# First block's norms in passes of high and low parts, with a buffer per tile; smaller sums, a swapped buffer and three moved waits in a decoder trunk

## The chip, the cores and the metric

The kernel runs on one core of a Trainium2 chip. The metric is the device time of one execution in microseconds (us), the median of several runs. Engines: PE (TensorE, matmul), DVE (VectorE), ACT (ScalarE), POOL (GpSimd) and SP (SyncE, which here only issues DMAs). Each has its own instruction stream; they meet at semaphores, each of which counts the finished instructions of one kind.

## The reference

One layer of a hybrid decoder trunk, in float32, over a prompt of 16 meta tokens and 2048 tokens, and over 8 samples of 4 tokens with a state each:

```python
h = rmsnorm(x, n1);  z = h @ w_in                       # 1024 -> 2560: u | q | f | i | gate
y_pool = pool_mix(z[..., :512])                         # window means 2, 4, 8, 16, then a product per group
y_rec = hgrn2_mix(z[..., 512:])                         # 4 heads of 128, chunked recurrence
x = x + concat(y_pool, y_rec) @ w_out
a, b = (rmsnorm(x, n2) @ w for w in (w_a, w_b))         # 1024 -> 2816
x = x + (gelu(conv3(a)) * b) @ w_down
y = rmsnorm(x, final_g)

def gla_chunk(S, q, k, g, v):                           # the recurrence of one chunk and head
    G = cumsum(g);  decay = exp(G[t] - G[s]) for s <= t
    A = einsum('td,sd,tsd->ts', q, k, decay)
    o = A @ v + (q * exp(G)) @ S
    S = exp(G[-1]) * S + (k * exp(G[-1] - G)).T @ v
```

Outputs are y of prompt and samples and the new states (pool, recurrent, convolution).

## The kernel before

**Blocks.** The prompt is worked in four blocks of 512 tokens, each of four tiles of 128. Block 0 (`hd` true, written out) also carries 48 head columns: the 16 meta tokens and the 32 sample tokens. Its 560 columns are split into a front (304: head and tiles 0 and 1) and a back (256: tiles 2 and 3), one PSUM bank each. Blocks 1 to 3 are a loop over the same code with `hd` false.

**Products in three parts.** A float32 product is made of reduced-precision parts: every operand is split in a high part (a cast) and a low part (value minus high), and PE does high x high, weight low x high, weight high x low (`three`, L558; `features`, L574, for a unit of eight k tiles). Weights come in 96 units of 128 x 1024 per block in four slots. In block 0 SP loads a unit raw, POOL splits it (L533 the high part, L536 the low), and SP stores the split to DRAM; later blocks load the split. A slot is loaded again once `unit_done` has counted the unit that used it.

**The norms.** ACT squares and sums the tokens, DVE and ACT make the reciprocal root, the tokens are scaled (`scaled`), PE transposes them (`row_transposes`, `token_rows`; L595), DVE multiplies the transposed tile by the gain out of PSUM into the buffer `t32` (L1608), ACT casts it to `h_hi` (L1145), and DVE subtracts for `h_lo` (L1616). There is one `t32` for all tiles and for the head, so a tile's multiply waits for the low part of the tile before. The head's counterparts are L603, L1630, L1150 and L1633. In block 0 the first user of the first norm is `first_gates` (L1085): the front halves of the four forget-gate units, unit by unit in three parts, then the back halves. The second norm's is `head_first` (L986), alike for the first four up-projection units. Both wait for tile 0's, tile 1's and the head's low parts before their first matmul.

**The gates.** DVE clamps each gate unit out of PSUM (L1730, L1731), ACT takes exponentials and logarithms, DVE cumulates (L1738 to L1743) and makes the keys; then come the decay operands, whose exponents DVE or, for heads 1 to 3 of block 0, POOL makes in the buffer `dec` (L378, L379).

**Attention.** 16 steps a block, a head and a tile each (`attention`, L737, L1953). For a step PE makes eight score matrices (L755, L758), DVE masks them (L1959) and adds the upper four to the lower four (L1965), PE multiplies the four sums by the values (L783), adds the state's share (L786) and the state's update (L789, whose keys ACT has copied, L1308, from a transpose, L771). DVE updates the state (L1975). A 128-column float32 product without split parts is two PE instructions. After certain steps PE does another unit: U and gate tiles (`gate_tile`, L819), pool products. Scores run two steps ahead; those of a head's first step wait for all its decay operands.

**Head states.** The samples' recurrent states of a head are loaded to one of two buffers `s0`, updated and stored (L1179). One buffer lies in the operands of odd heads, the other over `dec`; POOL's exponents of head 1 and ACT's first decays both wait for all four stores.

**Down projection.** Two halves of 512 columns. Each starts with the residual's add of what PE left in PSUM before (`half_residual`, L2024). In block 0, half 1 uses banks 3, 6, 7, 0 and 1; half 0 used 0, 1, 2, 5, 4. L1059 waits for the adds of tiles 0 and 1 (and the head) ahead of everything of half 1.

## Time and profile before

| | us |
| --- | --- |
| median of three runs (2640.07 to 2645.72) | 2641.01 |
| profiled execution, own time | 2635.29 |
| its span, first to last instruction | 2633.5 |
| PE busy | 2517.5 (96%) |
| DVE busy | 1178.2 (45%) |
| ACT busy | 714.2 (27%) |
| POOL busy | 450.8 (17%) |

The chain of work that ended last, followed back, is 88% PE, 6% DVE, 3% issue, 2% ACT and 1% DMA. The mean granted clock of PE is 0.985 of full speed. A row of a timeline gives start, duration, engine, line and operation, the count where several are merged, and in brackets the idle time before with what ended it. Matmuls are pipelined: their durations overlap, and what one costs is the distance of two starts. Between 30 and 34 us the granted clock is shown as 1.00 where the matmuls go at half pace; their distances are what is read there.

### The profile page before, as it was taken

To read this page: it belongs to the slowest core of one execution; us is meant where nothing else is said; L and a number is where in the kernel's file an instruction comes from. 1 tells how busy PE (TensorE), PEld (TensorE's weight loads), DVE (VectorE), ACT (ScalarE), POOL (GpSimd) and SP (SyncE) were. 2 spreads that over 40 slices of the span, in tenths; PEclk is the share of its full clock that TensorE was granted. 3 is DMA by queue.
4 is the path that set the end of the run, shared out by engine and by line. 5 is a ranking of instruction groups with operands and counts; after the bars stand their busy time and mean duration, and the time that the engine had idled before them with its cause. 6 is when DMAs were issued, how large, how long until landed. Compare 5 with 4: busy or idle time off the path is not lost.

```text
span 2633.5 us, 36805 instructions
## 1 busy us (share of the span) xinstructions
PE 2517.5 (96%) x13455; PEld 2135.5 (81%) x13455; DVE 1178.2 (45%) x2249; ACT 714.2 (27%) x1457; POOL 450.8 (17%) x331
## 2 busy tenths in 40 slices
PE   5997889999999999999999999999999999999997
PEld 5887779999777888888887887888887887888886
DVE  5977555333355764222236564322235764322234
ACT  3313222222323342211233332211133332211133
POOL 3625226555550120000000020000000020000000
PEclk9979989999999999999999999999999999999999
DMA  6641338777757423555656523455655622555653
GB/s 202 244 153 49 108 130 293 251 252 257 260 219 266 160 81 128 207 191 191 227 196 224 190 84 128 176 191 191 231 200 190 235 81 102 200 184 188 221 215 133
DMA packets 145354, 489.08 MB, mean 186 GB/s; under 512 B 8882, under 2 KB 79779, under 8 KB 96026
## 3 DMA queue, kind: packets, MB, share of 16 engines
q1 hardware_dynamic: 136747, 482.58, 50.5%
q10 hardware_dynamic: 8472, 4.75, 0.6%
q8 instruction: 80, 1.31, 0.2%
q14 instruction: 55, 0.44, 0.1%
HBM read 375.45 MB, written 112.02 MB: 185 GB/s over the span
## 4 chain that ended last, share of the span: by engine, by line
PE 88%; DVE 6%; issue 3%; ACT 2%; DMA 1%; POOL 0%; DVEq 0%; SPq 0%; ACTq 0%
PE ps L560 23%; PE ps L562 23%; PE ps L561 22%; PE ps L614 11%; PE ps L758 3%; PE ps L783 2%; PE ps L595 1%; DVE arena L1927 1%; DMA w_both<-w_split 1%; PE ps L789 1%; PE ps L755 0%; DVE arena L1959 0%; ACT arena L1157 0%; PE ps L840 0%; PE ps L786 0%
## 5 line engine op out<-in xcount | busy, mean ns | idle before, releaser
L560 PE MATMUL ps<-h_hi,w_both 128*128 128x512 f32 (+2 forms) x1664 | 626.6, 377 | 21.9 <-issue 13.5
L562 PE MATMUL ps<-h_lo,w_both 128*128 128x512 f32 (+2 forms) x1664 | 622.0, 374 | 0.0
L561 PE MATMUL ps<-h_hi,w_both 128*128 128x512 f32 (+2 forms) x1664 | 618.3, 372 | 0.0
L560 PEld LDWEIGHTS ps<-h_hi,w_both 128*128 128x128 f32 x1664 | 314.0, 189 | 78.2 <-issue 14.5
L562 PEld LDWEIGHTS ps<-h_lo,w_both 128*128 128x128 f32 x1664 | 314.1, 189 | 59.5
L561 PEld LDWEIGHTS ps<-h_hi,w_both 128*128 128x128 f32 x1664 | 314.5, 189 | 58.8
L560 PE MATMUL ps<-w_both,act_hi 128*128 128x512 f32 (+1 forms) x748 | 297.4, 398 | 4.3 <-DVE x_tok L2035 3.8
L562 PE MATMUL ps<-w_both,act_hi 128*128 128x512 f32 (+1 forms) x748 | 296.0, 396 | 0.0
L561 PE MATMUL ps<-w_both,act_lo 128*128 128x512 f32 (+1 forms) x748 | 295.6, 395 | 0.0
L614 PE MATMUL ps<-h_hi,w_both 128*128 128x304 f32 (+1 forms) x1664 | 290.2, 298 | 5.6 <-DVE arena L1731 2.4
L2112 DVE TENSOR_TENSOR act_lo<-arena,act_hi 128x512 fp32r<-128x512 f32 (+1 forms) x176 | 138.5, 789 | 331.3 <-ACT act_hi L1464 331.0
L378 POOL TENSOR_TENSOR arena<-arena 128x256 f32<-128x256 f32 x63 | 45.2, 717 | 1338.6 <-DVE arena L1927 1321.7
L614 PEld LDWEIGHTS ps<-h_hi,w_both 128*128 128x128 f32 x1664 | 241.9, 194 | 7.0 <-issue 2.6
L2072 DVE SCALAR_TENSOR_TENSOR arena<-arena,vec 128x512 f32<-128x512 f32 x88 | 69.2, 786 | 392.7 <-ACT arena L1390 391.9
L536 POOL TENSOR_TENSOR w_both<-w_raw,w_both 128x1024 fp32r<-128x1024 f32 x96 | 239.1, 2491 | 8.0
L1464 ACT CAST act_hi<-arena 128x512 fp32r<-128x512 f32 (+3 forms) x176 | 110.5, 630 | 352.7 <-PE ps L562 352.7
L560 PE MATMUL ps<-w_both,h_hi 128*128 128x512 f32 (+1 forms) x408 | 163.9, 402 | 17.8 <-issue 15.1
L614 PE MATMUL ps<-h_lo,w_both 128*128 128x304 f32 x832 | 177.0, 294 | 0.0
L533 POOL TENSOR_SCALAR w_both<-w_raw 128x1024 fp32r<-128x1024 f32 x96 | 112.4, 1170 | 356.7 <-DMA w_raw<-in_w_a 96.9
L560 PEld LDWEIGHTS ps<-w_both,act_hi 128*128 128x128 f32 (+1 forms) x748 | 138.3, 185 | 40.5 <-DVE x_tok L2035 4.3
L562 PEld LDWEIGHTS ps<-w_both,act_hi 128*128 128x128 f32 (+1 forms) x748 | 137.9, 184 | 36.3
L561 PEld LDWEIGHTS ps<-w_both,act_lo 128*128 128x128 f32 (+1 forms) x748 | 138.1, 185 | 35.3
(242 smaller groups left out, 3146.1 us busy)
## 6 DMA issues: line engine op xcount, KB each, us to landing
w_both<-w_split SPq DMA_DIRECT2D x288, 1024.0 KB, 4.8
w_split<-w_both SPq DMA_DIRECT2D x96, 1024.0 KB, 6.2
w_raw<-in_w_down SPq DMA_DIRECT2D x24, 512.0 KB, 4.2
w_raw<-in_w_a SPq DMA_DIRECT2D x22, 512.0 KB, 4.3
w_raw<-in_w_b SPq DMA_DIRECT2D x22, 512.0 KB, 4.2
w_raw<-in_w_in SPq DMA_DIRECT2D x20, 512.0 KB, 5.0
x_tok<-in_x_prompt SPq DMA_DIRECT2D x16, 512.0 KB, 6.9
arena<-in_x_prompt SPq DMA_DIRECT2D x16, 512.0 KB, 7.1
```

The costliest lines, as they stand in the source:

```text
L378: engine.tensor_tensor(o[:, :, 0:half], bb, gg[:, :, 0:half], ALU.subtract)
L533: nc.gpsimd.tensor_scalar(w_hi[:, s, :], w_raw[:, s, 0, :], 1.0, 1.0, ALU.mult, ALU.mult).then_inc(w_hi_ready, 1)
L536: nc.gpsimd.tensor_tensor(w_lo[:, s, :], w_raw[:, s, 0, :], w_hi[:, s, :].bitcast(F32), ALU.subtract).then_inc(w_ready, 1)
L560: nc.tensor.matmul(out, lhs[0], rhs[0], start=first, stop=False)
L561: nc.tensor.matmul(out, lhs[1], rhs[0], start=False, stop=False)
L562: return nc.tensor.matmul(out, lhs[0], rhs[1], start=False, stop=last)
L614: last = nc.tensor.matmul(out, lhs[:, k, :], rhs[:, k, cols], start=(k, n) == (0, 0), stop=(k, n) == (KD - 1, 2))
L758: last = nc.tensor.matmul(out, m, m, start=True, stop=True)
L783: nc.tensor.matmul(o, a_sum[:, win(l)], v_tok[:, w, hc], start=l == 0, stop=False)
L1464: nc.scalar.copy(act_hi[:, kk, lo:WIDE], acts[:, bass.ds(2 * i + kk, 1), lo:WIDE].rearrange("p a b -> p (a b)")).then_inc(act_hi_ready, 1)
L2072: own.mark(v.scalar_tensor_tensor(out=cv, in0=ae[:, 1:1 + BLOCK], scalar=w1, in1=cv, op0=ALU.mult, op1=ALU.add))
L2112: v.tensor_tensor(act_lo[:, kk, lo:WIDE], acts[:, bass.ds(2 * i + kk, 1), lo:WIDE].rearrange("p a b -> p (a b)"), act_hi[:, kk, lo:WIDE].b ...
```

## The change

- `t32_first` and `t32_head`: in block 0, each tile and the head have a buffer of their own for the transposed rows. `first_rows` multiplies, `first_low` and `head_low` subtract, as separate steps.
- `first_gates` and `head_first` do the high passes (16 matmuls a unit) for all four units, then the low passes (8 a unit); they wait for the high parts first and for the low parts only ahead of the low passes. The back of the last unit of `head_first` is done by itself, behind `hist_ready`. `unit_done` is counted in the low pass of the back. The transposes of tiles 2 and 3 stand ahead of the third unit, or behind the third and fourth.
- DVE's and ACT's order in both norms follows: multiplies of tiles 0 and 1, then squares, root and scalings of tiles 2 and 3, with the low parts of the head and of tiles 0 and 1 between or behind them.
- `s0`: the two buffers change places, and `rec_stored` is one semaphore per buffer. POOL's exponents of head 1 (L543) wait for the stores of heads 0 and 2 alone, ACT's first decays (L1326) for those of 1 and 3.
- Block 0, step 2: the gate tile stands ahead of scores(4).
- Down projection, half 1 of block 0: the wait for the residual stands ahead of tile 3 of the first k tile.
- Blocks 1 to 3: the four sums are added in place and again to two (`a_two`, two buffers by turns), so PE has two products with the values and not four, and the first addition has no wait for PE's use of the old sums.

Not shown in the diff are the renamed waits and calls that follow from these.

```diff
@@ -202,6 +202,10 @@
+t32_first = [part(D_MODEL * t, 2, 512) for t in range(TILES)]
+t32_head = part(D_MODEL * TILES, KD * HEAD)
@@ -225,6 +229,8 @@
+a_two = part(21086, 2, 2 * P)
@@ -234,7 +240,8 @@
-s0 = [part(17392, DEC_BATCH, P), part(19008, DEC_BATCH, P)]
...
+s0 = [part(19008, DEC_BATCH, P), part(17392, DEC_BATCH, P)]
...
@@ -577,6 +584,18 @@
+    def high_features(s, out, cols):
+        w = wslot(s, KD)
+        for k in range(KD):
+            nc.tensor.matmul(out, w[0][:, k, :], h_hi[:, k, cols], start=k == 0, stop=False)
+            nc.tensor.matmul(out, w[1][:, k, :], h_hi[:, k, cols], start=False, stop=False)
...
+    def low_features(s, out, cols):
+        w = wslot(s, KD)
+        for k in range(KD):
+            last = nc.tensor.matmul(out, w[0][:, k, :], h_lo[:, k, cols], start=False, stop=k == KD - 1)
@@ -779,8 +798,9 @@
-            for l in range((1 + LEVELS) // 2):
-                nc.tensor.matmul(o, a_sum[:, win(l)], v_tok[:, w, hc], start=l == 0, stop=False)
+            for l in range((1 + LEVELS) // 2 if hd else (1 + LEVELS) // 4):
+                nc.tensor.matmul(o, (a_sum if hd else a_two[:, i % 2, :])[:, win(l)], v_tok[:, w, hc], start=l == 0,
+                                 stop=False)
@@ -800,11 +820,15 @@
+            ahead = hd and i in GATE_BEHIND[1] and i == TILES - 2
+            if ahead:
...
+                gate_tile(b, hd, GATE_BEHIND[hd][i])
...
-            if i in GATE_BEHIND[hd]:
+            if i in GATE_BEHIND[hd] and not ahead:
@@ -985,24 +1009,37 @@
         def head_first():
...
+            pe.wait_ge(h_hi_ready, 2 * (4 + 2))
+            pe.wait_ge(hh_hi_ready, 3)
...
+            pe.wait_ge(t32_ready, 2 * (4 + 2))
+            pe.wait_ge(ht32_ready, 2)
+            fronts, backs = zip(*(up_banks(True, m // 2, m % 2) for m in range(4)))
+            for m in range(4):
+                pe.wait_ge(w_ready, U_UP + m + 1)
+                high_features(m, ps[:, fronts[m], 0:CUT], FRONT)
+                if m in (2, 3):
+                    token_rows(0, 1, m)
...
-                pe.wait_ge(w_ready, U_UP + m + 1)
-                features(m, ps[:, up_banks(True, m // 2, m % 2)[0], 0:CUT], FRONT)
-                if m in (1, 2):
-                    token_rows(0, 1, m + 1)
-            pe.wait_ge(h_ready, 2 * (4 + TILES))
+                low_features(m, ps[:, fronts[m], 0:CUT], FRONT)
+            pe.wait_ge(h_hi_ready, 2 * (4 + TILES))
+            pe.wait_ge(t32_ready, 2 * (4 + TILES))
...
-            for m in range(4):
-                if m == 3:
...
-                    pe.wait_ge(hist_ready, 1)
-                features(m, ps[:, up_banks(True, m // 2, m % 2)[1], HEAD:CUT], BACK).then_inc(unit_done, 1)
+            for m in range(3):
+                high_features(m, ps[:, backs[m], HEAD:CUT], BACK)
+            pe.wait_ge(h_ready, 2 * (4 + TILES))
+            for m in range(3):
+                low_features(m, ps[:, backs[m], HEAD:CUT], BACK).then_inc(unit_done, 1)
...
+            pe.wait_ge(hist_ready, 1)
+            high_features(3, ps[:, backs[3], HEAD:CUT], BACK)
+            low_features(3, ps[:, backs[3], HEAD:CUT], BACK).then_inc(unit_done, 1)
...
         def head_pair(j):
@@ -1044,6 +1081,9 @@
+                    if n and hd and first and t == 3:
...
+                        pe.wait_ge(x2_ready, 8 * b + 2)
@@ -1056,7 +1096,6 @@
-                pe.wait_ge(x2_ready, 8 * b + 2)
@@ -1089,17 +1128,27 @@
+        pe.wait_ge(h_hi_ready, 2 * 2)
+        pe.wait_ge(hh_hi_ready, 1)
+        pe.wait_ge(setup_done, 1)
+        for h in range(HEADS):
+            if h == 2:
+                row_transposes(0, 2, 0, 2)
+                row_transposes(0, 3, 2, 2)
+            weights(0, U_F + h, h, U_F // 4)
+            high_features(h, ps[:, two_banks(h)[0], 0:CUT], FRONT)
...
-        pe.wait_ge(setup_done, 1)
...
-            weights(0, U_F + h, h, U_F // 4)
-            features(h, ps[:, two_banks(h)[0], 0:CUT], FRONT)
-            if h < 2:
-                row_transposes(0, h + 2, 2 * h, 2)
+            low_features(h, ps[:, two_banks(h)[0], 0:CUT], FRONT)
+        pe.wait_ge(h_hi_ready, 2 * TILES)
...
+        pe.wait_ge(t32_ready, 2 * TILES)
+        for h in range(HEADS):
+            high_features(h, ps[:, two_banks(h)[1], HEAD:CUT], BACK)
...
-            features(h, ps[:, two_banks(h)[1], HEAD:CUT], BACK).then_inc(unit_done, 1)
+            low_features(h, ps[:, two_banks(h)[1], HEAD:CUT], BACK).then_inc(unit_done, 1)
@@ -1139,15 +1188,16 @@
-    def rows_hi(n, t):
+    def rows_hi(n, t, own_buffers=False):
+        buf = t32_first[t] if own_buffers else t32
...
-                           t32[:, half, :].rearrange("p (k n) -> p k n", k=4)).then_inc(h_hi_ready, 1)
+                           buf[:, half, :].rearrange("p (k n) -> p k n", k=4)).then_inc(h_hi_ready, 1)
...
     def head_hi(w):
...
-        nc.scalar.copy(h_hi[:, :, 0:HEAD], t32[:, 0, 0:KD * HEAD].rearrange("p (k n) -> p k n", k=KD)
+        nc.scalar.copy(h_hi[:, :, 0:HEAD], t32_head.rearrange("p (k n) -> p k n", k=KD)
...
     def decays(b, h, steps):
...
@@ -1323,7 +1373,7 @@
-                act.wait_ge(rec_stored, 16 * HEADS)
+                act.wait_ge(rec_stored[1], 16 * HEADS // 2)
...
@@ -1534,14 +1584,13 @@
+    rows_hi(0, 0, True)
+    rows_hi(0, 1, True)
+    head_hi(0)
...
-    act.wait_ge(x_loaded[2], 16)
-    square(x_tok, 2, 2)
-    rows_hi(0, 0)
-    act.wait_ge(x_loaded[3], 16)
-    square(x_tok, 3, 3)
-    rows_hi(0, 1)
-    head_hi(0)
+    for t in range(2, TILES):
+        act.wait_ge(x_loaded[t], 16)
+        square(x_tok, t, t)
...
@@ -1618,18 +1668,36 @@
+    def first_rows(n, w, t, banks):
...
+        for half in range(2):
+            dve.wait_ge(xt_done, 2 * (n + t) + half + 1)
+            v.tensor_tensor(t32_first[t][:, half, :].rearrange("p (k n) -> p k n", k=4),
+                            ps[:, banks[half], :].rearrange("p (k n) -> p k n", k=4),
+                            gain[w][:, 4 * half:4 * half + 4].unsqueeze(2).broadcast_to([P, 4, P]),
+                            ALU.mult).then_inc(t32_ready, 1)
...
+    def first_low(n, t):
+        for half in range(2):
+            dve.wait_ge(h_hi_ready, 2 * (n + t) + half + 1)
+            v.tensor_tensor(h_lo[:, 4 * half:4 * half + 4, main(t)],
+                            t32_first[t][:, half, :].rearrange("p (k n) -> p k n", k=4),
+                            h_hi[:, 4 * half:4 * half + 4, main(t)].bitcast(F32),
+                            ALU.subtract).then_inc(h_ready, 1)
...
     def head_scaled(w):
...
     def head_rows(w):
-        x = (1, 3)[w]
-        dve.wait_ge(hxt_done, x)
-        dve.wait_ge(h_ready, 2 * (TILES if w else 2))
-        th = t32[:, 0, 0:KD * HEAD].rearrange("p (k n) -> p k n", k=KD)
+        dve.wait_ge(hxt_done, (1, 3)[w])
+        th = t32_head.rearrange("p (k n) -> p k n", k=KD)
...
-        dve.wait_ge(hh_hi_ready, x)
...
+    def head_low(w):
+        th = t32_head.rearrange("p (k n) -> p k n", k=KD)
+        dve.wait_ge(hh_hi_ready, (1, 3)[w])
...
     def gate_bounds():
@@ -1654,15 +1722,18 @@
-        rows(0, 0, x_tok, 0, 0, False)
-        rows(0, 0, x_tok, 1, 2, False)
+        first_rows(0, 0, 0, (0, 1))
+        first_rows(0, 0, 1, (2, 3))
...
+        first_low(0, 0)
...
-        dve.wait_ge(hh_ready, 1)
-        rows(0, 0, x_tok, 2, 0, False)
-        rows(0, 0, x_tok, 3, 2, False)
+        first_low(0, 1)
+        head_low(0)
+        first_rows(0, 0, 2, (0, 1))
+        first_rows(0, 0, 3, (2, 3))
+        first_low(0, 2)
+        first_low(0, 3)
...
     def residual_and_norm(b, hd):
@@ -1703,9 +1774,11 @@
-                dve.wait_ge(hh_ready, 3)
...
-            rows(n, 1, x_tok, t, banks[t], False)
+            if hd:
+                first_rows(n, 1, t, banks[t])
+            else:
+                rows(n, 1, x_tok, t, banks[t], False)
@@ -1715,6 +1788,15 @@
+        if hd:
+            head_low(1)
+            first_low(n, 0)
+            first_low(n, 1)
+            for t in range(2, TILES):
+                first_rows(n, 1, t, banks[t])
+            for t in range(2, TILES):
+                first_low(n, t)
+            return
@@ -1959,10 +2041,16 @@
-            if not (isinstance(n, int) and n == 0):
...
-                dve.wait_ge(o_done, n)
-            v.tensor_tensor(a_sum, a_all[:, 0:4 * P], a_all[:, 4 * P:8 * P], ALU.add).then_inc(at_ready, 1)
+            if hd:
+                if n:
+                    dve.wait_ge(o_done, n)
+                v.tensor_tensor(a_sum, a_all[:, 0:4 * P], a_all[:, 4 * P:8 * P], ALU.add).then_inc(at_ready, 1)
+                return
+            own.mark(v.tensor_tensor(a_all[:, 0:4 * P], a_all[:, 0:4 * P], a_all[:, 4 * P:8 * P], ALU.add))
+            own.settle()
+            dve.wait_ge(o_done, n - 1 if i else n)
+            v.tensor_tensor(a_two[:, i % 2, :], a_all[:, 0:2 * P], a_all[:, 2 * P:4 * P], ALU.add).then_inc(
+                at_ready, 1)
...
```

## Rows read from the trace of the kernel before

**Rows 1.** Timeline of all engines, 18 to 60 us (start, duration, engine, line, operation).

```profile
18.19 1.08 PE L603 MATMUL ps<-tab,arena 48*128 48x48 f32 x8
...
27.07 2.65 POOL L536 TENSOR_TENSOR w_both<-w_raw,w_both 128x1024 fp32r<-128x1024 f32 x1
...
27.63 0.56 DVE L1630 TENSOR_TENSOR arena<-ps,vec 128x384 f32<-128x384 f32 x1
...
28.22 0.51 ACT L1150 CAST h_hi<-arena 128x384 fp32r<-128x384 f32 x1 [3.04 <-DVE arena L1630]
...
30.24 0.59 PE L560 MATMUL ps<-h_hi,w_both 128*128 128x304 f32 x1 [10.97 <-issue]
...
54.59 0.79 DVE L1738 SCALAR_TENSOR_TENSOR arena<-arena,lb 128x560 f32<-128x560 f32 x1
```

**Rows 2.** Timeline of PE, first block's attention, around step 2.

```profile
209.50 0.80 PE L755 MATMUL ps<-arena 128*128 128x128 f32 x2 [3.25 <-DVE arena L1927]
...
210.09 3.19 PE L758 MATMUL ps<-arena 128*128 128x128 f32 x14
```

**Rows 3.** Timeline of all engines, second norm, 354 to 406 us.

```profile
354.95 2.93 DVE L1600 TENSOR_SCALAR arena<-x_tok,norms 128x1024 f32<-128x1024 f32 x1
...
355.00 2.34 POOL L536 TENSOR_TENSOR w_both<-w_raw,w_both 128x1024 fp32r<-128x1024 f32 x1
...
357.81 1.27 DVE L1608 TENSOR_TENSOR arena<-ps,vec 128x512 f32<-128x512 f32 x2
...
364.37 2.34 POOL L536 TENSOR_TENSOR w_both<-w_raw,w_both 128x1024 fp32r<-128x1024 f32 x1
...
367.92 0.62 PE L560 MATMUL ps<-h_hi,w_both 128*128 128x304 f32 x1 [8.46 <-DVE h_lo L1616]
...
394.39 1.05 POOL L533 TENSOR_SCALAR w_both<-w_raw 128x1024 fp32r<-128x1024 f32 x1 [27.68 <-DMA w_raw<-in_w_a]
...
405.01 0.75 PE L614 MATMUL ps<-h_hi,w_both 128*128 128x304 f32 x4 [0.56 <-DVE arena L2095]
```

**Rows 4.** Timeline of PE at two restarts after a wait.

```profile
325.44 0.40 PE L560 MATMUL ps<-w_both,h_hi 128*48 128x512 f32 x1 [2.11 <-issue]
...
729.83 0.50 PE L560 MATMUL ps<-w_both,act_hi 128*128 128x512 f32 x1 [3.78 <-DVE x_tok L2035]
```

**Rows 5.** Busy time by stretch (us, busy and instructions per engine, clock, DMA, GB/s).

```profile
30.20:34.20 4.00, 3.96 (x16) 3.99 (x17) 0.67 (x5) 2.60 (x4) 0.00 (x0) 1.00 0.00 0
...
47.20:58.80 11.60, 11.60 (x98) 11.41 (x96) 7.09 (x12) 5.41 (x8) 3.19 (x2) 1.00 0.62 213
...
729.80:733.80 4.00, 3.97 (x11) 3.15 (x12) 2.07 (x6) 0.00 (x0) 3.35 (x3) 0.60 0.72 298
...
893.00:986.00 93.00, 87.51 (x573) 76.62 (x572) 57.67 (x98) 34.12 (x97) 19.09 (x26) 1.00 0.22 80
```

**Rows 6.** Chain that ended last, by time (start, us, what), the two gate tiles.

```profile
213.29 7.13 PE ps L614 x48
...
239.51 6.19 PE ps L614 x48
```

**Rows 7.** Timeline of PE, one attention step of the second block.

```profile
900.58 1.06 PE L783 MATMUL ps<-arena 128*128 128x128 f32 x8
...
901.47 0.39 PE L786 MATMUL ps<-state,arena 128*128 128x128 f32 x2
```

**Rows 8.** Waits of the whole span (who waited for whom: us, times, longest).

```profile
PE ps L789 <- ACT arena L1308: 12.5, 14, 1.5
...
PE ps L771 <- DVE state L1975: 8.1, 8, 1.6
...
POOL arena L378 <- DMA out_rec_sample<-arena: 17.0, 1, 17.0
```

**Rows 9.** Groups by form, DVE, 893 to 986 us (busy, mean ns, idle before).

```profile
L1965 DVE TENSOR_TENSOR arena<-arena 128x512 f32<-128x512 f32 x14 | 11.2, 798 | 20.6 <-PE ps L786 20.3
...
L1926 DVE TENSOR_TENSOR arena<-arena 128x256 f32<-128x256 f32 x14 | 5.9, 419 | 10.2 <-ACT arena L1157 10.2
```

More of the change, by code:

```diff
@@ L297, in trunk_step @@
         v_seq_ready, hs_done, hs_ready, rec_stored = (
-            sem("v_seq_ready"), sem("hs_done"), sem("hs_ready"), sem("rec_stored"))
+            sem("v_seq_ready"), sem("hs_done"), sem("hs_ready"), [sem(f"rec_stored{i}") for i in range(2)])
         ovar_ready, oguess_ready, y_ready, yt_done, y_hi, y_taken = (
@@ L541, in ahead @@
                     if h == 1:
-                        pool.wait_ge(rec_stored, 16 * HEADS)
+                        pool.wait_ge(rec_stored[0], 16 * HEADS // 2)
                     for i in range(1 + LEVELS):
@@ L579, in features @@
                                  k == 0, k == KD - 1)
+                return last
+            def high_features(s, out, cols):
[7 more added lines that the diff above has]
+                    last = nc.tensor.matmul(out, w[0][:, k, :], h_lo[:, k, cols], start=False, stop=k == KD - 1)
                 return last
@@ L1368, in body @@
                 root_guess(var[:, 1:2], rstd[:, 1:2], var2_ready, 3 * b + 2, guess2_ready)
-                rows_hi(8 * b + 4, 0)
-                rows_hi(8 * b + 4, 1)
+                rows_hi(8 * b + 4, 0, hd)
+                rows_hi(8 * b + 4, 1, hd)
                 tile_square(2)
@@ L1373, in body @@
                 root_guess(var[:, 2:TILES], rstd[:, 2:TILES], var2_ready, 3 * b + 3, guess2_ready)
-                rows_hi(8 * b + 4, 2)
-                rows_hi(8 * b + 4, 3)
+                rows_hi(8 * b + 4, 2, hd)
+                rows_hi(8 * b + 4, 3, hd)
                 nc.scalar.preload_act_table(ACT.Gelu)
@@ L1551, in _ @@
             for t in range(2, TILES):
-                rows_hi(0, t)
+                rows_hi(0, t, True)
             act.wait_ge(setup_done, 1)
@@ L1566, in _ @@
             act.wait_ge(hout_ready, 17)
-            act.wait_ge(rec_stored, 16 * HEADS)
+            for r in rec_stored:
+                act.wait_ge(r, 16 * HEADS // 2)
         @block.vector
@@ L2191, in _ @@
             body(0, 1)
-            with own.loop(1, BLOCKS, 106) as b:
+            with own.loop(1, BLOCKS, 122) as b:
                 body(b, 0)
```

4 lines of the change are left out of this document (2 added, 2 removed).

## The prediction

> **What bounds the kernel now.** I read the page first: TensorE (PE) is busy 96% of the span and carries 88% of the chain that ended last; VectorE (DVE) carries 6% of it, ScalarE (ACT) 2%. So two things pay: work taken from PE, and waits of PE. The waits of the whole span come next, then the timeline around each edit. PE stands still before the first features, 10.97 us, until the head's low parts are there [rows 1]; 3.25 us in the first block's attention [rows 2]; 8.46 us before the second norm's features [rows 3]; 3.78 us for the residual in the down projection [rows 4]. In blocks 1 to 3 it hardly waits: 87.5 busy of 93 us around an attention, DVE 57.7 [rows 5]. There the kernel is bound by PE's instructions, in block 0 by hand-offs.
>
> All times below are in the profiled execution: span 2633.5, its own time 2635.3. The median shown is 2641.0; I take the sum off that.
>
> **A. First norm (block 0).** Before: PE starts at 30.24, on tile 1's and the head's low parts. After: it needs only high parts. The head's transposes end at 19.27, its multiply takes 0.56, its cast 0.51 [rows 1]; with hand-offs PE starts at 20.7. The high passes of four units are 64 matmuls of 304 columns: 16 at half pace, 4.0 us [rows 5]; 48 at 0.14 (0.118 for 256 columns, from 98 in 11.6 us [rows 5], times 304/256), 6.8; the transposes of tiles 2 and 3 take 2. That is 33.5, and late enough for the fourth unit's weights, split at 29.72 [rows 1], and for the low parts, which DVE finishes near 31 beside GpSimd (POOL). Low passes: 32 x 0.14 = 4.5, to 38. Back half: 64 high x 0.118 = 7.6, to 45.6; then 0.94 a unit. Units 0 and 1 are done at 46.5 and 47.5; before, unit by unit, at 50.1 and 53.0 (47.26 + 24 x 0.118 each). So of the 9.5 us by which PE starts early, 3.8 are given back because a unit now ends after all four high passes. Behind it the gates' chain is DVE's: before it started 1.6 after unit 1 (54.59 [rows 1]); after, the clamps of unit 0 and 1 stand behind each other (1.6 each) and ACT's logarithms take 2.3: 46.5 + 1.6 + 2.3 = 50.3 to 50.4. Gain 4.2. Bounds: 0 (the chain keeps its time by collisions with POOL) and 9.5 (the whole early start).
>
> **B. Gate tile ahead of the scores (block 0, step 2).** PE waits 3.25 until 209.50, then does scores(4) on the low clock, 16 instructions in about 3.5 [rows 2], then the gate tile, 7.13 against 6.19 warm [rows 6]. After: gate tile at 206.25, ends 212.5, the operands are there since 209.5, scores warm 16 x 0.11 = 1.8 [rows 7]: 214.4 in place of 220.4. Gain 6.0; 3.9 if the clock falls at 206 all the same (2 us for 4 us at half pace). I take 5.5. Nobody is starved: DVE's masked sum for the step stood waiting for PE.
>
> **The state buffers swapped, the stores' semaphore split.** POOL's exponents of head 1 wait 17.0 us for the last store [rows 8] and now only for heads 0 and 2. But ACT, which consumes them, comes to them after step 0 and still waits for the odd heads' stores. 0, bounds -0.5 and +0.5 (POOL moves beside another DVE instruction).
>
> **C. Second norm.** Before: tile 0's low parts stand between the multiplies of tiles 0 and 1 (multiply at 357.81, start of features 367.92) and a scaling takes 2.93 beside POOL [rows 3]. After: the multiplies follow each other and the head's low part is gone from before them; PE starts near 358. It isn't worth 10 us, for three reasons. Units 2 and 3 are split only at 362.8 and 366.71 (364.37 + 2.34 [rows 3]). The low parts now stand behind the adds, root and scalings of tiles 2 and 3: the last scaling ends 0.5 after the split, 367.2, head low 0.56, four halves at 0.64 [rows 1, 3]: 370.3. From there 32 low matmuls 4.5, history transposes 1.5, three units' back high passes 48 x 0.118 = 5.7, the first low pass 0.9: unit 0 is released at 382.9, in place of 389.6. The next unit's split begins 4.8 after a release (394.39 [rows 3]) and takes 3.5: ready at 391.2, while PE is through with unit 3 at 387.7 and stands 3.5 us, after which it restarts low (7.1 to 8.2 for the wide unit against 6.2 [rows 6]). So the next unit starts at 399.5 in place of 405.01 [rows 3]. Gain 5.5; bounds 0 (weights, not norms, set the pace throughout) and 9.6.
>
> The Trainium skill, SBUF — State Buffer, section "SBUF: two separate sides", has the port pair that DVE and GpSimd share as a lock held for a whole instruction, the loser "fully blocks". The trace agrees for POOL's subtraction: the 2.93 us scaling ends 0.5 after it, at 357.88 [rows 3]. By that rule a scaling of tile 3 that gets in before 364.37 would hold POOL off instead: low parts some 0.6 earlier, the fourth split as much later, the sum 29.8 to 31.0 in place of 30.4.
>
> **D. Residual.** PE stops at 726.05 and starts at 729.83; of the next 4 us most are at the low clock, mean 0.60 [rows 4, 5]. After: the first three tiles, 9 x 0.23 = 2.1, run at once, a wait of 1.7 remains, and the low clock should not come: after a 2.11 us wait at 325.44 it did not [rows 4]. 2.1 + 1.5 = 3.6; bounds 2.1 and 3.8.
>
> **E. Attention of blocks 1 to 3.** Each of 16 steps has two products fewer, four instructions x 0.111 (eight from 900.58 to 901.47 [rows 7]) = 0.445; 48 steps: 21.4. DVE adds one addition of 256 elements, 0.42 [rows 9], about 0.45 with the hand-off. It has 35 us free in such a stretch, and of the old addition's wait 20.3 us were for PE [rows 9]; that wait goes. But PE's saving is lost where it then waits for another: for ACT's copy of the keys (14 waits, 12.5 us in all [rows 8], three per such block, about two more copies come within 0.3 us of being late) and once per block for DVE's state (1.6). Six steps lose their 0.445, and in the one behind DVE the new addition costs 0.6: 7.1 - 2.7 - 0.6 = 3.9 a block, 11.6 in three. Bounds: +21.4 and, with the addition on the path of every step, 48 x 0.45 = -21.6.
>
> Sum: 4.2 + 0 + 5.5 + 5.5 + 3.6 + 11.6 = 30.4 us, 2641.0 to 2610.6; I say 2610.5, own range 2604 to 2618.
>
> **Rivals.**
> 1. E pays nothing: what PE drops, it waits for ACT or DVE. For it: the copies above. Against: in ten of 16 steps no wait ends near. 30.4 - 11.6 = 18.8: 2622. 14%.
> 2. A and C pay nothing: weights and the DVE chain keep their times (late release of the slots, collisions with POOL). For it: 3.8 of 9.5 go that way even in my sum. 30.4 - 9.7 = 20.7: 2620. This holds the case that the early pass doesn't happen at all. 11%.
> 3. Everything passes through: A 4.2, B 6, C 7, D 3.8, E 21.4 = 42.4: 2598.6. 9%.
> 4. The other side: DVE's addition decides. Place: the sum behind every mask in blocks 1 to 3; price 0.86 us where POOL works on the same port (the old addition took up to twice its time there; mean 798 ns against 0.69 [rows 9]); 48 x 0.86 = 41.3, less the 18.8 of A to D: 2663.5. It decides from (18.8 + 5.3)/48 = 0.50 us per step on the path; at 0.45 it ends at 2643.8, no change. Against: DVE is idle 38% there. 3%, and 4% for no change.
>
> The forecast has 59%. A measurement of this kernel can tell some 0.2%, 5.3 us, from none. Faster 0.93, same 0.04, slower 0.03. The range, 2599 to 2626, takes in rivals 1 and 2 and ends at 3.
>
> **What would show it.** A: PE's first feature near 20.7, DVE's first cumulation near 50.3. B: no wait of DVE's operands behind step 2, a gate tile of 6.2. C: a start near 358, low passes at 370, a new wait of about 3.5 for POOL's split, the next wide unit near 5.5 earlier than A and B explain. D: a residual wait of 1.7, granted clock 1.0 behind it. E: a block (601.3 us before, the same transposes of step 11 at 957.85 and 1559.17) of 597.4; the waits for ACT's copies longer. The forecast is wrong if a block takes 600 or more (rival 1), if the gates' chain starts later than 53, or if DVE's sums release PE in most steps (rival 4).

## The result and the profile after

The changed kernel takes 2626.7 us (median of six runs, 2621.75 to 2628.76) against 2640.55 for the kernel before in the same series: ratio 0.9947, 95% interval 0.9932 to 0.9962. It is faster, by 14 us and not by the 30 predicted; 2626.7 lies just above the range. The profiled execution of the changed kernel took 2626.98 us, span 2625.2, mean granted clock 0.981 (before 2635.29, 2633.5, 0.985). The chain of the end is still 88% TensorE (PE).

Below, marks that the prediction named and some more, in both profiles and in a second profile of the kernel before, taken later (us from the span's start):

| mark | before | before, again | after | forecast |
| --- | --- | --- | --- | --- |
| PE's first feature | 30.24 | 31.13 | 20.68 | 20.7 |
| gates' chain starts on VectorE (DVE) | 54.59 | 55.91 | 57.00 | 50.3 |
| first key transpose, block 0 | 192.8 | 195.6 | 198.0 | |
| head transposes, second norm | 347.8 | 353.4 | 353.1 | |
| first wide unit behind the second norm's four | 398.1 | 400.2 | 397.6 | |
| first key transpose, block 1 | 887.7 | 888.9 | 883.4 | |
| a block, first key transpose to the next (two in each profile) | 601.3, 602.6 | 601.4, 601.6 | 599.8, 601.6 | 597.4 |

The kernel before lies 0.9 to 5.6 us apart with itself inside block 0. What the changed kernel gains is therefore read from stretches, over as many profiles as there are, and not from the difference of two marks.

The timeline of the changed kernel, first norm, PE, then ScalarE (ACT), DVE and GpSimd (POOL) (start, duration, line, operation, idle before). It answers to [rows 1]:

```profile
20.68 0.38 PE L592 MATMUL ps<-h_hi,w_both 128*128 128x304 f32 x1 [1.24 <-ACT h_hi L1195]
31.01 3.67 PE L614 MATMUL ps<-tab,arena 128*128 128x128 f32 x16 [5.63 <-ACT arena L1569]
...
29.81 2.19 ACT L1569 ACTIVATE arena<-x_tok,norms 128x1024 f32<-128x1024 f32 x2 [3.19 <-DVE norms L1641]
...
12.22 0.17 DVE L1628 TENSOR_SCALAR norms<-norms 128x5 f32<-128x5 f32 x1 [2.63 <-ACT arena L1181]
23.82 2.33 DVE L1628 TENSOR_SCALAR norms<-norms 128x2 f32<-128x2 f32 x1
27.37 2.21 DVE L1637 TENSOR_SCALAR norms<-norms 128x2 f32<-128x2 f32 x1
53.12 0.47 DVE L1812 TENSOR_SCALAR arena<-ps 128x304 f32<-128x304 f32 x1 [15.30 <-PE ps L598]
57.00 0.80 DVE L1820 SCALAR_TENSOR_TENSOR arena<-arena,lb 128x560 f32<-128x560 f32 x1 [0.94 <-ACT arena L1270]
...
23.45 2.68 POOL L543 TENSOR_TENSOR w_both<-w_raw,w_both 128x1024 fp32r<-128x1024 f32 x1
27.22 2.34 POOL L543 TENSOR_TENSOR w_both<-w_raw,w_both 128x1024 fp32r<-128x1024 f32 x1
```

PE starts where the forecast had it, does two units' high passes and then stands 5.63 us for the scaling of tile 2; the 16 transposes behind the wait take 3.3 us at the low clock, where the prediction had 2. The scaling waits for the root of tiles 2 and 3, five DVE instructions on 128 x 2 numbers. The first of them takes 0.17 us at 12.22; at 23.82 it takes 2.33, and at 27.37 the fourth takes 2.21. Both end when a POOL subtraction (L543) does: 23.45 + 2.68 and 27.22 + 2.34. Before, the same root ran behind POOL's last split.

Second norm and down projection, from the timelines of PE and POOL; they answer to [rows 3, 4]:

```profile
362.99 0.41 PE L592 MATMUL ps<-h_hi,w_both 128*128 128x304 f32 x1 [1.62 <-ACT h_hi L1195]
372.33 1.09 PE L614 MATMUL ps<-tab,arena 128*128 128x128 f32 x8 [2.37 <-DVE arena L1650]
397.60 1.00 PE L633 MATMUL ps<-h_hi,w_both 128*128 128x304 f32 x4 [3.46 <-POOL w_both L543]
729.54 0.51 PE L567 MATMUL ps<-w_both,act_hi 128*128 128x512 f32 x1 [1.76 <-DVE x_tok L2123]
...
394.07 1.05 POOL L540 TENSOR_SCALAR w_both<-w_raw 128x1024 fp32r<-128x1024 f32 x1 [22.34 <-DMA w_raw<-in_w_a]
395.20 2.34 POOL L543 TENSOR_TENSOR w_both<-w_raw,w_both 128x1024 fp32r<-128x1024 f32 x1
```

The wait of 3.46 us for POOL's split and the residual's wait of 1.76 are those forecast (3.5 and 1.7).

An attention of a loop block, first to last key transpose, in windows (length, busy time and instructions by engine, granted clock, DMA share, GB/s): before, then changed. This is a narrower cut than [rows 5].

```profile
887.70:979.70 92.00, 87.72 (x582) 77.81 (x580) 58.27 (x99) 31.75 (x91) 19.09 (x26) 1.00 0.23 84
```

```profile
883.40:972.90 89.50, 82.89 (x526) 72.00 (x525) 66.03 (x114) 31.67 (x91) 19.10 (x26) 1.00 0.24 86
```

And PE's waits in it, before and changed (us in total, times, longest; compare [rows 8], which are of the whole span):

```profile
PE ps L789 <- ACT arena L1308: 2.1, 3, 0.8
PE ps L771 <- DVE state L1975: 1.6, 1, 1.6
```

```profile
PE ps L809 <- ACT arena L1358: 3.8, 5, 1.1
PE ps L790 <- DVE state L2063: 2.1, 1, 2.1
```

The columns of the windows are PE, its weight loads, DVE, ACT and POOL. The stretch holds 14 of the 16 steps. Their 56 instructions fewer are worth 6.2 us at 0.11 each; PE is busy only 4.83 us less, because the matmuls right beside its waits last 1.3 us longer in sum. The stretch is 2.6 us shorter: 1.7 go to longer waits for ACT's copies of the keys, 0.5 to a longer one for DVE's state. Up to PE's second restart behind the attention, with all 16 steps, it is 3.1 us: 114.3 to 114.5 us from the first key transpose to there in all nine attentions of the three profiles with the old sums, 111.3 to 111.4 in the sixteen with the new sums inside which the clock stayed up.

Right behind such a stretch, at the second restart ("issue", 2 us idle), PE's windows of the changed kernel and then of the one before:

```profile
994.70:998.70 4.00, 3.96 (x11) 0.58 0.00 0
```

```profile
1002.00:1006.00 4.00, 3.92 (x17) 1.00 0.02 4
```

11 matmuls of 512 columns in 4 us against 17: the granted clock, 0.58 of full speed, is near its lower level, 1.2 of 2.4 GHz. From the restart (1002.08 and 994.74) to the next wait's end (1018.27 and 1012.55) PE takes 16.2 us before and 17.8 after: the fall costs 1.6 us. The kernel before shows the same price by itself: behind its second attention the clock falls too, and the same stretch takes 17.8 us there.

Inside an attention the clock falls at one place only, behind PE's wait for DVE's state. PE before, then the changed kernel's second loop block:

```profile
915.19 0.30 PE L771 MATMUL ps<-tab,arena 128*128 128x128 f32 x1 [1.61 <-DVE state L1975]
```

```profile
1510.30 0.30 PE L790 MATMUL ps<-tab,arena 128*128 128x128 f32 x1 [2.08 <-DVE state L2063]
...
1511.00:1512.00 1.00, 1.00 (x7) 0.50 0.00 0
```

### The profile page after: what moved, and what is told of

Its sections match the earlier page's. It is cut to its first block, busy times and chain, and to the rows that moved or that the text cites. A ratio compares the mean times of both kernels' runs of the same rounds, so it can differ in the third digit from the quotient of the medians.

```text
span 2625.2 us, 36506 instructions
## 1 busy us (share of the span) xinstructions
PE 2509.0 (96%) x13263; PEld 2122.3 (81%) x13263; DVE 1200.8 (46%) x2297; ACT 713.7 (27%) x1457; POOL 450.6 (17%) x331
## 4 chain that ended last, share of the span: by engine, by line
PE 88%; DVE 6%; issue 2%; ACT 2%; DMA 1%; POOL 0%; DVEq 0%; SPq 0%; ACTq 0%
PE ps L567 22%; PE ps L569 22%; PE ps L568 22%; PE ps L633 11%; PE ps L777 3%; PE ps L614 1%; PE ps L809 1%; PE ps L802 1%; DMA w_both<-w_split 1%; PE ps L913 0%; PE ps L774 0%; PE ps L598 0%; PE ps L592 0%; PE ps L864 0%; DVE arena L2041 0%
## 5 line engine op out<-in xcount | busy, mean ns | idle before, releaser
L567 PE MATMUL ps<-h_hi,w_both 128*128 128x512 f32 (+1 forms) x1536 | 586.8, 382 | 2.9 <-issue 2.9
L569 PE MATMUL ps<-h_lo,w_both 128*128 128x512 f32 (+1 forms) x1536 | 583.2, 380 | 0.0
L568 PE MATMUL ps<-h_hi,w_both 128*128 128x512 f32 (+1 forms) x1536 | 579.6, 377 | 0.0
L569 PEld LDWEIGHTS ps<-h_lo,w_both 128*128 128x128 f32 x1536 | 288.5, 188 | 59.6
L568 PEld LDWEIGHTS ps<-h_hi,w_both 128*128 128x128 f32 x1536 | 288.8, 188 | 58.9
L567 PEld LDWEIGHTS ps<-h_hi,w_both 128*128 128x128 f32 x1536 | 288.2, 188 | 58.7 <-issue 3.7
L633 PEld LDWEIGHTS ps<-h_hi,w_both 128*128 128x128 f32 x1664 | 245.0, 196 | 11.5 <-issue 6.0
L543 POOL TENSOR_TENSOR w_both<-w_raw,w_both 128x1024 fp32r<-128x1024 f32 x96 | 238.7, 2486 | 8.0
L1514 ACT CAST act_hi<-arena 128x512 fp32r<-128x512 f32 (+3 forms) x176 | 110.5, 630 | 347.8 <-PE ps L569 347.8
```

Of the source, the lines that this page charges most:

```text
L543: nc.gpsimd.tensor_tensor(w_lo[:, s, :], w_raw[:, s, 0, :], w_hi[:, s, :].bitcast(F32), ALU.subtract).then_inc(w_ready, 1)
L567: nc.tensor.matmul(out, lhs[0], rhs[0], start=first, stop=False)
L568: nc.tensor.matmul(out, lhs[1], rhs[0], start=False, stop=False)
L569: return nc.tensor.matmul(out, lhs[0], rhs[1], start=False, stop=last)
L633: last = nc.tensor.matmul(out, lhs[:, k, :], rhs[:, k, cols], start=(k, n) == (0, 0), stop=(k, n) == (KD - 1, 2))
L1514: nc.scalar.copy(act_hi[:, kk, lo:WIDE], acts[:, bass.ds(2 * i + kk, 1), lo:WIDE].rearrange("p a b -> p (a b)")).then_inc(act_hi_ready, 1)
```

## The experiments

Each was timed against the kernel before on the same chip, twelve profiles in three series; the series ran on three different chips, with medians of before of 2639.6, 2638.1 and 2640.5 us. Every ratio is to before. The changed kernel itself (ratio 0.9947) is in none of the three. A distance from it is therefore given twice: from the medians, and in brackets from the two ratios times 2640 us. The interval of one ratio is 0.09 to 0.15% to either side, that of such a distance some 5 us. No single mend is well clear of that by its time alone, so each is settled by the profile.

### The sums alone

```diff
 # the kernel before, with
+own.mark(v.tensor_tensor(a_all[:, 0:4 * P], a_all[:, 0:4 * P], a_all[:, 4 * P:8 * P], ALU.add))
+v.tensor_tensor(a_two[:, i % 2, :], a_all[:, 0:2 * P], a_all[:, 2 * P:4 * P], ALU.add)
```

> The kernel before with the attention sums of blocks 1 to 3 alone (two products with the values a step, a second addition on VectorE, two buffers by turns). Theory, from the two traces: a step is shortened, an attention phase of a loop block takes some 3.1 us less (89.4 instead of 91.9 us between the first and last key transposes, and a little behind them), but TensorE has less to do in it, and at the restart behind the phase its granted clock falls to the lower level for some 4 us, which gives back 1.6 us; so the kernel gains 4 to 5 us in all, ratio to before 0.9983, and the low stretches show at about 980 to 1000, 1580 to 1600 and 2180 to 2200 us. Rival, the prediction's own term: 3.9 us a block that nothing gives back, 11.6 us, ratio 0.9956. Second rival: the sums pay nothing or cost, ratio 1.000 or above.

Measured: 2634.3 us, ratio 0.9978 (0.9969 to 0.9987), 5.3 us. The phases took 91.0, 90.9 and 89.4 us, and the clock fell behind each, and inside the first two. The first theory holds but for the falls inside, which it did not have; the prediction's 11.6 us lies outside the interval (3.4 to 8.2).

### Four products again

```diff
-for l in range((1 + LEVELS) // 2 if hd else (1 + LEVELS) // 4):
+for l in range((1 + LEVELS) // 2):   # window l % 2 in blocks 1 to 3: each sum is used twice, the output is too large
```

> The changed kernel, but TensorE does four products with the values again in blocks 1 to 3 (the two sums twice over, so the attention output is too large there); VectorE's two additions stay. Theory: what the sums save is TensorE's two products a step, so here a phase takes as long as in the kernel before or up to 2 us longer (the second addition is then paid for), but the clock does not fall behind it; against the changed kernel +9 us from the phases less some 5 us of low clock, +4 to +6 us, ratio to before about 0.997. Rival: the gain came from the removed wait for the old sums (two buffers), then the phase stays at 89.4 us and the kernel is 5 us faster than the changed one, ratio 0.993 or below.

Measured: 2634.8 us, 0.9981 (0.9971 to 0.999), 8 us slower than the changed kernel (by the ratios 9), more than the 4 to 6 expected. The phase with the clock up:

```profile
2094.30:2186.80 92.50, 87.76 (x582) 77.84 (x581) 66.00 (x114) 31.77 (x91) 19.10 (x26) 1.00 0.24 84
```

92.5 us, 0.5 more than before: all of the gain is PE's two products, none the removed wait, and the second addition costs 0.5 a phase. That is PE's wait for DVE's state, 2.08 us here against 1.61. In the other two phases (94.1 us) the clock fell behind this wait. One point of the theory was wrong: the clock fell behind all three phases here too, with as much work for PE as before.

### GpSimd held behind the root

```diff
+if isinstance(j, int) and j == 0 and s == 2:
+    pool.wait_ge(roots_ready, 2)
```

> The changed kernel with one wait more: GpSimd splits the third and fourth weight unit only once the roots of tiles 2 and 3 are ready. Theory: the root's instructions on 128 x 2 numbers stood behind GpSimd's split instructions (2.33 and 2.21 us where the same ones take 0.16), which made the scaling of tile 2 start at 29.81. Without that the root ends at about 24.5, tile 2 is scaled from 24.6, its transposes stand at 26, the splits of units 2 and 3 end at 28.4 and 31.8, the front halves end at 40 instead of 44.3, and the gates' chain on VectorE starts at 52.5 to 53 instead of 57.0; 4 to 4.5 us off the kernel, if the chain stays VectorE's up to 130 us. Rival A: the start of the chain is set by the late release of the units (all low passes of the back halves last), then the root is quick but the chain starts at 55 or later. Rival B: the squares or the units' splits are late, then the scaling of tile 2 starts before 26 but the third unit waits for GpSimd beyond 31 and nothing is won.

Measured: 2620.3 us, 0.9927 (0.9915 to 0.994), 6.4 us under the changed kernel (5.3). DVE and POOL:

```profile
23.20 0.17 DVE L1630 TENSOR_SCALAR norms<-norms 128x2 f32<-128x2 f32 x1 [0.21 <-ACT arena L1179]
24.26 0.17 DVE L1639 TENSOR_SCALAR norms<-norms 128x2 f32<-128x2 f32 x1
52.24 0.80 DVE L1822 SCALAR_TENSOR_TENSOR arena<-arena,lb 128x560 f32<-128x560 f32 x1 [0.94 <-ACT arena L1272]
...
24.80 1.35 POOL L542 TENSOR_SCALAR w_both<-w_raw 128x1024 fp32r<-128x1024 f32 x1 [2.96 <-DVE norms L1643]
```

The root is through at 24.6 (29.8 in the changed kernel), the chain starts at 52.24 instead of 57.00 as expected, and the first key transpose stands at 191.6 (198.0). Rival A, the late release alone, would have kept the chain at 55.

### Back halves unit by unit, first norm

```diff
-for h in range(HEADS): high_features(h, ..., BACK)
+pe.wait_ge(h_ready, 2 * TILES)
-for h in range(HEADS): low_features(h, ..., BACK).then_inc(unit_done, 1)
+for h in range(HEADS): features(h, ..., BACK).then_inc(unit_done, 1)
```

> The changed kernel, but the back halves of the four gate units go unit by unit in all three parts, as before the change (the front halves keep the passes). Theory of the late release: the back halves start at 44.3 as now, unit 0 is done at 47.2 instead of 53.0, the clamps of head 0 start there and the gates' chain starts at about 51.2 instead of 57.0; but its first 15 us then meet GpSimd's next splits, so 3 to 5 us of it are left at 100 us and in the whole kernel (ratio to the changed kernel 0.998 to 0.999). Rival: the chain is paced by GpSimd's collisions and not by its start, then less than 1 us is left at 100 us.

Measured: 2619.1 us, 0.9925 (0.9913 to 0.9937), 7.6 us under the changed kernel (5.8), more than expected. DVE:

```profile
47.48 0.47 DVE L1810 TENSOR_SCALAR arena<-ps 128x304 f32<-128x304 f32 x1 [9.50 <-PE ps L569]
51.70 1.59 DVE L1818 SCALAR_TENSOR_TENSOR arena<-arena,lb 128x560 f32<-128x560 f32 x1
```

The clamps start 5.6 us and the chain 5.3 us earlier; the root is as slow as in the changed kernel (2.35 and 2.21 us). The first key transpose is at 191.5. Behind it the moved gate tile ran with the clock up, which gives this profile 3.2 us more that the mend does not touch. So the passes, which were to help PE, held each unit back until all four were nearly done, and DVE was waiting for the first.

### The first norm undone

```diff
 # first_gates, first_norm and ACT's order as before the change, t32 for the rows
```

> The changed kernel with the first norm undone: its order on TensorE, VectorE and ScalarE and its one buffer for the rows are those of the kernel before (the head keeps a buffer of its own); all else stays. Theory: this part of the change is a loss, the gates' chain starts at 54.6 again instead of 57.0 and the first key transpose of the attention at about 193 instead of 198.0, so the kernel is some 5 us faster than the changed one (about 2621.5, ratio to before 0.9928). Rival: the 5 us at 190 come from the swap of the sample states' buffers and GpSimd's earlier exponents; then the chain starts at 54.6 but the key transpose stays at 196 or later and the kernel at 2625 or more.

Measured: 2623.1 us, 0.9934 (0.992 to 0.9947), 3.6 us under the changed kernel (3.4); the chain starts at 54.37, the first key transpose is at 196.1. The ratios' intervals overlap, so the time alone shows no loss. Over the profiles the first key transpose stands at 192.8 to 196.1 in the four with the old first norm (mean 195.2) and at 196.7 to 198.0 in the six with the new one unmended (mean 197.6): a loss of 2.4 us at that mark, where 5 were expected. The rival's "196 or later" holds for the mark, but neither its time nor its cause.

### The gate tile behind the scores again

```diff
-ahead = hd and i in GATE_BEHIND[1] and i == TILES - 2
+ahead = False
```

> The changed kernel with the gate tile of step 2 behind the scores again. Read from the two traces, the tile ahead gave 3.3 us (5.1 us late at 190, 1.7 us late at 222) and not the 5.5 of the prediction, since the tile then ran on the lower clock (8.62 us). So this kernel is 3 to 3.5 us slower than the changed one, the attention of block 0 is 3.3 us longer (84.2 to 87.5 between the first and the last key transpose). Rival: with the chain as late as in the changed kernel the tile's place is worth nothing, since what TensorE gains there it gives back at the next wait for VectorE's operands; then the phase is 84 to 85.

Measured: 2630.8 us, 0.9966 (0.9951 to 0.998), 4.1 us over the changed kernel (5.0). Block 0's phase is 87.7 us against 84.2. The gate tile on the chain (start, duration), here and in the changed kernel:

```profile
218.23 7.25 PE ps L633 x48
```

```profile
211.70 8.62 PE ps L633 x48
```

Ahead of the scores the tile begins 6.5 us sooner and runs 1.4 longer, on the lower clock: 3.5 us in these two, not 5.5. But the clock falls under the moved tile only in some profiles. In no_residual, whose code is the same up to there, it stayed up:

```profile
210.13 6.17 PE ps L633 x48
```

The phase took 84.2 us in the three profiles in which the low clock lasted longest, 82.3 in two, and 80.9 or 81.0 in five, the tile taking 6.17 us there. Without the moved tile it took 86.8 to 87.7 in four. The means are 82.2 and 87.2: the part gave 5.0 us, and 6.3 where the clock stayed up.

### Back halves unit by unit, second norm

```diff
-for m in range(3): high_features(m, ..., BACK)
+pe.wait_ge(h_ready, 2 * (4 + TILES))
-for m in range(3): low_features(m, ..., BACK).then_inc(unit_done, 1)
+for m in range(3): features(m, ..., BACK).then_inc(unit_done, 1)
```

> The changed kernel, but in the second norm the back halves of the first three units go unit by unit in all three parts. In the changed kernel the first unit's slot is released at 389.4 us, its reload takes 4.3 us and GpSimd's split 3.5, and TensorE waits for it until 397.6 while its own work ends at 393. Theory: the first unit is done 4 us earlier, the split ends at 393.5, TensorE goes on at once: 3.5 to 4 us less, here and in the whole kernel. Rival: the reload waits for something else (the DMA engines are busy with the stores of the splits), then TensorE still starts the wide units at 396.5 or later.

Measured: 2620.5 us, 0.9931 (0.9917 to 0.9945), 6.2 us under the changed kernel (4.2). POOL's next split:

```profile
389.59 1.05 POOL L540 TENSOR_SCALAR w_both<-w_raw 128x1024 fp32r<-128x1024 f32 x1 [18.30 <-DMA w_raw<-in_w_a]
390.73 2.40 POOL L543 TENSOR_TENSOR w_both<-w_raw,w_both 128x1024 fp32r<-128x1024 f32 x1
```

It begins 4.5 us earlier and the first wide unit starts at 393.5 instead of 397.6: 4.1, as expected, and what the ratios give. The other 2 us of the median are the difference of two series.

### All three mends

> The changed kernel with the three mends together: GpSimd's split of the third and fourth unit behind the roots, and the back halves unit by unit in both norms. If the three effects add (6.4, 7.6 and 4 us): 2609, ratio to before 0.988. If the two of the first norm share one cause, GpSimd's splits beside VectorE's chain, the second adds little to the first: 2615, ratio 0.9905. Theory says between: the back halves start 4.7 us earlier than in the kernel with the unit-by-unit back halves alone, so the gates' chain starts at 47 to 48 against 51.7, but GpSimd's next splits come as much earlier.

Measured: 2607.5 us (2606.3 to 2610.0), 0.9881 (0.9866 to 0.9896), 19 us under the changed kernel (17). The three apart give 20 by the medians (15 by the ratios): within the noise they add. This is the fastest version, and beats both kernels. DVE:

```profile
43.41 0.48 DVE L1810 TENSOR_SCALAR arena<-ps 128x304 f32<-128x304 f32 x1 [7.67 <-PE ps L571]
47.62 1.58 DVE L1818 SCALAR_TENSOR_TENSOR arena<-arena,lb 128x560 f32<-128x560 f32 x1
```

The chain starts at 47.6 (57.0 in the changed kernel), the first key transpose is at 185.5 (198.0), the first wide unit at 380.2 (397.6).

### The mended kernel without the sums, and three controls

```diff
 # fixed_no_sums: all_fixed with one addition and four products a step
```

> The kernel with all three mends (2607.5 us) without the attention sums of blocks 1 to 3. Theory: the sums are worth 4.5 to 5.5 us there as in the kernel before (2.6 us a phase, of which 1.6 go back to the lower clock behind it), so 2612 to 2613, with block periods of 601.3 to 602 us instead of 600.5 and no fall of the clock behind two phases of three. Rival, the prediction's term: 11.6 us, 2619.

Measured: 2613.4 us, 0.9906 (0.9891 to 0.9921): the sums are worth 5.9 us there (6.6), as the theory had it within the noise.

> The kernel before once more, for a second profile. The kernel with the attention sums alone has the same instructions as the kernel before in block 0, and yet its first key transpose stood at 196.1 us against 192.8, its head transposes of the second norm at 353.9 against 347.8 and its first wide unit of the up projection at 404.1 against 398.1. Theory: the profiled execution of before was an early one, and a second profile shows marks between the two, nearer 196, 353 and 403. Rival: the two are alike (192.8, 347.8, 398.1 to 0.5 us) and something in the sums' kernel reaches block 0. For the clock: with the sums TensorE's granted clock fell behind the attention phase of a loop block in each of nine profiles; if the sums are the cause it stays up here behind at least two phases of three, as in the first profile of before.

Measured (one run): 2637.3 us. The marks are 195.6, 353.4 and 400.2: the first profile of before was an early one up to the second norm. The third mark does not show it: 400.2 lies between 398.1 and the 404.1 of sums_only. Of its 5.6 us at the second mark, 3.5 arise between the last key transpose and the head transposes (67.4 us against 70.9), where DVE's low parts of y met a POOL split or missed it. The first two marks are within 0.6 us of those of sums_only, so nothing of the sums needs to have reached into block 0 up to there. The clock fell behind one attention of three.

```diff
 # no_swap
-s0 = [part(19008, DEC_BATCH, P), part(17392, DEC_BATCH, P)]
+s0 = [part(17392, DEC_BATCH, P), part(19008, DEC_BATCH, P)]   # both waits for all four stores
```

> The changed kernel with the two buffers of the samples' states in their old places and both waits for all four stores again. The prediction gave this part nothing. Theory: nothing in the whole kernel (within 1.5 us of 2626.7), the first key transpose within 1 us of 198.0. Rival: GpSimd's earlier exponents of head 1 are what slowed VectorE and TensorE between 130 and 190 us in the changed kernel; then the key transpose comes at 195.5 or earlier and the kernel is 2 us faster or more.

Measured: 2623.1 us, 0.9942 (0.9927 to 0.9956), first key transpose at 197.2. No effect that can be told from none; the median is 3.6 us lower (by the ratios 1.3), and the profile had the early y stretch (67.4 us) and the clock up under the gate tile, which the swap does not touch.

```diff
 # no_residual: the wait back ahead of half 1
```

> The changed kernel with the wait for the residual's adds ahead of everything of half 1 again. Read from nine profiles, the stretch from the down projection's first product to the first key transpose of block 1 took 241.3 us with the old wait and 236.7 to 239.0 with the new one, which is 2.4 us of waiting and, in four of the eight, 2 more because the clock did not fall behind the wait. So here the stretch is 241.3 and the kernel 2.4 to 4.6 us slower, about 2630. Rival: the wait is hidden in the changed order, the stretch stays below 239.5 and the time at 2627.

Measured: 2628.3 us, 0.9956 (0.9944 to 0.9969), 1.6 us over the changed kernel (2.4). The stretch from the down projection's first product to the first key transpose of block 1 took 241.7 us, the wait 3.77:

```profile
724.85 0.80 PE L567 MATMUL ps<-w_both,act_hi 128*128 128x512 f32 x1 [3.77 <-DVE x_tok L2121]
...
724.00:728.00 4.00, 3.15 (x7) 0.50 0.92 358
```

With the wait ahead the stretch was 241.3 to 241.7 us in four profiles; with it moved, 236.7 to 237.1 in five and 238.5 to 239.0 in five, the mean 237.9: 3.5 us on average.

### The clock behind the attention, over all profiles

In windows of 2 us over each attention of a loop block and the 32 us behind it: in the three profiles without the second addition (two of before, one of fixed_no_sums) the granted clock fell below 0.9 behind 3 of 9 attentions and inside none; in the eleven with it, behind 33 of 33 and inside 16. Each of the 16 falls inside begins at the end of PE's wait for DVE's state or within 1.5 us of it. That wait is 2.07 or 2.08 us in all 33 attentions with the second addition and 1.61 or 1.62 in the nine without. Behind the attention PE's two restarts have the same idle time with and without it (1.7 and 1.97 us). With the two products, an attention with no fall inside took 89.4 us, one with it 90.9 to 91.1.

## Why the prediction was wrong

By the stretches and the times the terms came out as follows. Their sum is 16 us, against the 14 measured with an interval of some 4 us to either side; each term is uncertain by 1 to 2.

| term | forecast | measured | from |
| --- | --- | --- | --- |
| A first norm | +4.2 | -2.4 | first key transpose, 197.6 against 195.2, means of six and four profiles; medians -3.6 |
| B gate tile | +5.5 | +5.0 | phase 87.2 and 82.2, means of four and ten profiles; medians 4.1, ratios 5.0 |
| s0 swap | 0 | 0 | swap undone |
| C second norm | +5.5 | +4.5 | head transposes to wide unit: 50.4, 46.8, 50.2 without, 44.0 to 46.0 with, the second norm unmended |
| D residual | +3.6 | +3.5 | fourteen profiles |
| E sums | +11.6 | +5.5 | medians 5.3 and 5.9; the periods of the profiles give 3.5 |

**A, the step "That is 33.5".** It let the transposes of tiles 2 and 3 take 2 us inside the high passes, as if their scaling were ready; it was not until 30.9 (transposes from 31.01, after a wait of 5.63 us), and the high passes ended at 39.7 instead of 33.5. I had charged POOL's port for DVE's large instructions, but not for the root's tiny ones, which DVE now issues among POOL's splits. The front halves ended at 44.3 instead of 38. The late release was then added to it: the prediction named it at 3.8, its sum holds 5.1 (38 to 50.4 us instead of the 7.3 of before), and it came as 5.3. Each of the two is shown by its mend: 4.8 us and 5.3 us at the chain's start, 9.4 together. The Trainium skill, SBUF — State Buffer, section "SBUF: two separate sides", calls the shared port pair an "exclusive lock" and has whichever instruction starts first keep it for its whole length; for a DVE instruction of 128 x 2 that stood 2.3 us beside POOL's subtraction, the trace agrees: POOL's two subtractions had begun 0.37 and 0.15 us before. The prediction had quoted that very rule, for the scaling alone; there the profile has the scaling 0.05 us ahead of POOL (354.95 and 355.00 [rows 3]) and it was held all the same, so starts this close do not tell in a profile who goes first. What I called rival 2 was thus half right: true of A, worse than its zero, and untrue of C.

**E, the step "3.9 a block".** Two errors. The saving itself is 3.1 a block: of the 7.1 that the products are worth, the waits took 4.0 where the step had 3.3. There are five waits for ACT's key copies in place of three, 1.7 us more, 0.5 more for DVE's state, and the matmuls beside the waits last longer, which the step left out. Then the clock: a fall behind each attention costs 1.6 us, and in half of them one inside costs 1.6 more. That is what the prediction did not have at all: it took E's stretches, at full clock before, to stay there. Per block, 3.1 less 1.6 x (1 - 1/3) less 1.6 x 1/2 is 1.2, and the blocks of the profiles give 1.2 (600.7 us over the periods with the sums, 601.8 without); the medians give 1.8 to 2. What pulls the clock down is known in part. The two products fewer do not, since with four it falls as well. The falls inside begin behind the wait for DVE's state, which the second addition makes longer, 2.08 us instead of 1.61; with that wait the clock falls in 16 of 33, and no run has the second addition without the longer wait. Why it falls behind every attention, and behind a third of them without the addition, is open.

**B** is right, to 0.5 us. In the first profile it lost 1.4 us to the lower clock under the moved tile, for which the lower bound of 3.9 stood; in five of ten profiles it did not. **C and D** were right in mechanism and nearly in size; the new wait for the split, 3.5 us, came as forecast. The prediction's 405.01 is the start of the second wide unit. From the head transposes to there it is 53.0 to 57.2 us in the three profiles with the old second norm (mean 55.6) and 51.8 to 53.0 in eight with the new one (mean 52.3): 3.3 us at that mark, and part of the 5.5 was that the profile of before was the latest of its three there. In D, in four of the ten profiles with the residual's wait moved, the clock fell behind it all the same (0.57 to 0.66 over the next 4 us), which the step had ruled out. A fifth, no_first, had as long a stretch with the clock up, which is not explained.

Of the marks set down beforehand, these spoke against the forecast: the chain later than 53, a block of 600 or more (one of the two in the first profile, most in the others), and, in the first profile alone, a gate tile of 8.6 instead of 6.2.

## What to carry to other kernels

Before DVE work is moved to where GpSimd works, price its smallest instructions too: each can stand for a whole GpSimd instruction, and a chain of five meets two. Passes over several units start the first engine sooner but deliver every unit late; where the consumer takes them one by one, finish them one by one, and use the passes only in the part where the inputs are late. A saving read off PE's instruction count in a stretch at full clock must be checked against the waits next to it and against the clock behind it. And profile both kernels more than once, if single marks are to be compared: the gate tile's gain reads 3.5 us from one pair of profiles and 5.0 from fourteen.

## What was not expected of the hardware

A DVE instruction of 128 x 2 numbers took 2.2 to 2.35 us beside a GpSimd subtraction, 0.17 without. The granted clock fell behind 33 of 33 attentions with a second DVE addition and behind 3 of 9 without, PE busy 87.8 of 92.5 us in one (with four products) and 87.7 of 92.0 in the other; inside the attentions it fell only behind a wait of 2.08 us, in 16 of 33, and never behind the same wait of 1.61. Identical instructions of block 0 lay up to 5.6 us apart in two profiles.
